# Five chunks accumulated per slice over unnormalised activations, with the root applied as the banks are copied

## The chip, the cores and the metric

The kernel runs on one core of a Trainium2 chip. The metric is the device time in microseconds of one execution, lower is better; a profile comes from one execution of its own.

## What is computed

Two transformer blocks on x of 256 tokens by 1024, float32. What concerns this change is the beginning of the first one:

```python
mod = c @ ada_w[l] + ada_b[l]
sh1, sc1, gt1, sh2, sc2, gt2 = [m[:, None, :] for m in jnp.split(mod, 6, axis=-1)]
h = rmsnorm(x, norm1_g[l]) * (1.0 + sc1) + sh1
p = h @ w_in[l]                       # 1024 -> 7168
xr, yr, q, k, v, ga, gb = jnp.split(p, cuts, axis=-1)
...
q = head_rmsnorm(q.reshape(b_, s_, ATT_HEADS, HEAD_DIM), q_norm_g[l])
k = head_rmsnorm(k.reshape(b_, s_, ATT_HEADS, HEAD_DIM), k_norm_g[l])
y_b = stick_breaking_attention(q, k, v)
```

rmsnorm divides each token's row by its root r = sqrt(mean(x^2) + eps). Behind these lines come a gated recurrence beside the attention, an output projection, a gated feed forward layer, and the second block: two attentions and 32 experts of two layers, of which each token takes four.

## The kernel before

Activations lie transposed: 1024 features as 8 slices k of 128 partitions, 256 tokens along the free side (`xT`, `hT`). Weights come in pieces of up to 1 MB through a ring of 17 slots; the SyncE queue issues the transfers in the order of `plan`, and each waits until the piece 17 places earlier has been used. c, the constants and the column vectors are issued by ScalarE's queue.

The order on every engine is written out by hand, and semaphores join them. At the start, ScalarE squares x, VectorE adds the squares, TensorE sums them over the features (L581), and ScalarE takes the root. For each slice k VectorE multiplies a piece of the modulation weights by c and sums it, one half for the shift and one for the scale (`first_modulation`, L1941), and multiplies x by the reciprocal root (L1946); ScalarE makes scale and shift of them and applies both (L1425), which is slice k of `hT` and raises `h`. TensorE then adds this slice's share to four chunks at once, the **slab** (L589): chunks ("qk", 0) to ("qk", 3), the eight heads' q, each 256 columns wide and in a bank of its own. Each later chunk is computed whole over the eight slices (`chunk`, L569): k in ("qk", 4) to ("qk", 7), then conv, v, gel and so on. This list is `main`; a chunk's place in it decides its bank and whom it waits for:

```python
n = self.main_at[key]
if n >= 3:
    _, sem, value = K.main[n - 3]
    e.wait_ge(sem, value)            # the chunk three places earlier is copied out
```

Every q and k chunk n is normalised by head: VectorE copies the bank (`qk_copy`, L1998), ScalarE squares it (L1433), TensorE sums (`qk_norm`, L612), ScalarE takes the root (L1439), VectorE takes the reciprocal (L2003) and multiplies (`qk_scale`, L2007 or L2009, and L2011 for q's factor 128^-0.5). VectorE's order is: copies 0, 1 and 2, scaling 0, copy 3, scaling 1, copy 4, scaling 2, some 128x8 operations of a softplus, copy 5, and so on. TensorE's attention scores of head 0 (L627) wait for all eight scalings.

The expert weights stream through the same ring at the end; their first transfers (L498) wait for the last pieces of the layers before them.

Of the kernel before, what the change touches and what calls it, by code (L numbers as in the profile page):

```python
# [15 lines left out]
S = 256  # L16
# [128 lines left out]
class Board:  # L145
# [36 lines left out]
    def lay_scratch(self):  # L182
# [16 lines left out]

        self.lt = [self.modc[:, 1, 8 * n:8 * n + 8] for n in range(5)]  # L200
        self.sq1 = [carve(512) for _ in range(4)]
        self.rst1 = carve(256)
        place[0] = 0
        self.qk = [carve(8, 256), carve(8, 256)]
        self.vv = carve(2, 1024)
        self.mix = carve(8, 256)
        self.Wt = [carve(512) for _ in range(10)]
        self.xp = carve(2, 260)
        self.xcs = [self.Wt[0], carve(512)]
# [78 lines left out]
    def lay_pieces(self):  # L288
# [10 lines left out]

        for k in range(8):  # L300
            ada(0, [k])
            plan.append((("slab", k), a["slab"][k], 1024))
        for n in range(4, 8):
            w_in(("qk", n), 8 + n)
        w_in(("conv", 0), 0)
        for c in range(4):
# [39 lines left out]
        self.done_at, n = {}, 0  # L346
        for key, _, _ in plan:
            if key == ("slab", 7):
                for c in range(4):
                    self.done_at[("qk", c)] = n + c + 1  # L350
                n += 3
            if key[0] not in ("b1", "ada"):
                n += 1
                self.done_at[key] = n
# [86 lines left out]
        return self.bank[3 if x == NE - 1 else 2]  # L441

    def main_bank(self, key):
        return self.bank[5 if key == ("qk", 3) else self.main_at[key] % 3]

    def second_bank(self, key):
        return self.bank[self.second_at[key] % 7]
# [12 lines left out]

    def modulation(self, i):

        return {0: (0, 0, "norm1", self.rst1), 1: (0, 24, "norm2", self.rst), 2: (1, 0, "pre_mix", self.rst),
                4: (1, 24, "pre_ffn", self.rst)}[i]


def sync_program(e, K):
# [86 lines left out]
def tensor_program(e, K):  # L554
# [28 lines left out]
    for k in range(8):  # L583
        v = landed(("slab", k))
        e.wait_ge(S.h, k + 1)
        for c in range(4):
            for j in range(2):
                o0 = c * 256 + j * 128
                ins = mm(K.main_bank(("qk", c))[:, 256 * j:256 * j + 256], v[:, o0:o0 + 128], K.hT[:, k, :],  # L589
                         start=(k == 0 and j == 0), stop=(k == 7), skip_group_check=True)  # L590
            if k == 7 or c == 3:
                ins.then_inc(S.piece_done, 1)
    e.wait_ge(S.ld_con2, 16)

# [9 lines left out]
    def chunk(key, h=None):  # L604
        v, b = main(key)
        tiles2(v, K.hT, b, h).then_inc(S.piece_done, 1)
# [4 lines left out]
            e.wait_ge(S.qk_rt, n - 1)  # L611
        mm(B[3 + n % 2][:, :], ones, K.Wt[2 * (n % 2)], start=True, stop=True).then_inc(S.qk_sum, 1)  # L612

    for n in range(4, 8):
        chunk(("qk", n))
        for m in range(2 * n - 8, 2 * n - 6):
            if m == 7:
                chunk(("conv", 0))
            qk_norm(m)

    def att_scores(h):
        b, q, k = B[3], K.qk[0][:, h, :], K.qk[1][:, h, :]
# [34 lines left out]
    for c in range(4):  # L657
        v, b = main(("v", c))
        for tt in range(2):
            for k in range(8):  # L660
                ins = mm(b[:, 256 * tt:256 * tt + 256], K.hT[:, k, tt * 128:(tt + 1) * 128],  # L661
                         v[:, k * 256:(k + 1) * 256], start=(k == 0), stop=(k == 7))
        ins.then_inc(S.piece_done, 1)
        chunk(("gel", c))
        att_step(2 * c)
        if c < 3:
            chunk(("conv", c + 1))
            att_step(2 * c + 1)
        rg = landed(("rg", c))
        e.wait_ge(S.xc, c + 1)  # L670
        if c:
            e.wait_ge(S.rg_th, c)
        xc = K.xcs[c % 2]
        for j in range(2):
            mm(B[5][:, 256 * j:256 * j + 256], rg[:, j * 128:(j + 1) * 128], xc[:, 256 * j:256 * j + 256], start=True,
               stop=True)
# [690 lines left out]
def scalar_program(e, K):  # L1367
# [31 lines left out]
                scale=K.mc[:, k:k + 1]).then_inc(S.h, 1)  # L1399


    e.dma_start(K.cb[:, :], a["cb1"]).then_inc(S.ld_cb, 16)
    e.dma_start(K.con[:, 0:256], a["consts"][:, 0:256]).then_inc(S.ld_col, 16)
    e.dma_start(K.col[:, :], a["cols"]).then_inc(S.ld_col, 16)
    e.wait_ge(S.consts, 3)
# [6 lines left out]
    e.wait_ge(S.act, done.n)  # L1412
    act(K.lt[0], K.lt[0], ACT.Exp, scale=-1.0).then_inc(S.coef, 1)
    table(ACT.Sqrt)
    norm_root(0, K.rst1)
    e.wait_ge(S.gain, 1)
    for k in range(8):
        e.wait_ge(S.ada_sum, 2 * k + 1)
        act(K.mc[:, 8 + k:9 + k], K.modc[:, 0, k:k + 1], ACT.Identity, bias=C("ada_b", k)).then_inc(S.act, done.one())
        e.wait_ge(S.ada_sum, 2 * k + 2)  # L1420
        act(K.mc[:, k:k + 1], K.modc[:, 0, 8 + k:9 + k], ACT.Identity, bias=K.mc[:, 16 + k:17 + k],
            scale=C("norm1", k)).then_inc(S.act, done.one())
        e.wait_ge(S.hn, k + 1)
        e.wait_ge(S.act, done.n)
        act(K.hT[:, k, :], K.hT[:, k, :], ACT.Identity, bias=K.mc[:, 8 + k:9 + k],  # L1425
            scale=K.mc[:, k:k + 1]).then_inc(S.h, 1)


    def qk_square(n):
# [426 lines left out]
def vector_program(e, K):  # L1856
# [69 lines left out]
    e.wait_ge(S.vec, done.n)  # L1926
    tt_(K.sq1[0][:, 0:256], K.sq1[0][:, 0:256], K.sq1[0][:, 256:512], ALU.add).then_inc(S.vec, done.one())
    e.wait_ge(S.ld_col, 32)
    stt(K.mc[:, 16:24], C("ada_b", 8, 8), 1.0, C("norm1", 0, 8), ALU.add, ALU.mult).then_inc(S.gain, 1)

    def first_modulation(k):

        i = K.at[("ada", 0, k)]
        v = K.piece(("ada", 0, k))
        for j in range(2):
            if k == 0 and j == 0:
                e.wait_ge(S.ld_ada, 16)
            else:
                e.wait_ge(S.ring[i % RING], 16 * (i // RING + 1))
            m, w = 8 * j + k, v[:, 1024 * j:1024 * j + 1024]  # L1940
            ins = stt(w, w, 1.0, K.cb[:, :], ALU.mult, ALU.mult, accum_out=K.modc[:, 0, m:m + 1])  # L1941
            ins.then_inc(S.ada_sum, 1)

    def first_scaled(k0, k1):
        for k in range(k0, k1):
            tt_(K.hT[:, k, :], K.xT[:, k, :], K.rst1, ALU.mult).then_inc(S.hn, 1)  # L1946

    e.wait_ge(S.ld_cb, 16)
    first_modulation(0)
    norm_end(0, K.rst1)  # L1950
    e.wait_ge(S.rstd, 1)
    first_scaled(0, 2)
    for k in range(1, 8):
        first_modulation(k)
        if k < 4:
            first_scaled(2 * k, 2 * k + 2)
    e.sem_inc(S.mod, 1)
    e.wait_ge(S.ld_con2, 16)

# [874 lines left out]
def lay_out(i):  # L2834
# [83 lines left out]
```

## Time and profile before

| | us |
|---|---|
| median of 3 runs | 1613.96 |
| lowest and highest | 1612.82, 1615.13 |
| the profiled execution | 1614.23 |
| its span, first to last instruction | 1612.3 |
| TensorE busy in it | 1558.4 (97%) |
| VectorE busy | 656.5 (41%) |
| ScalarE busy | 340.6 (21%) |

In the rows PE is TensorE, PEld its weight loads, DVE VectorE, ACT ScalarE, SP SyncE; q marks an engine's queue. Times count from the span's start. "a<-b" is output and inputs by their names in the program, and what stands in brackets at a row's end is the engine's idle time ahead of it and what ended it. TensorE's products are pipelined and their ends modelled, so the distance from start to start is the better measure. An f32 product appears as two instructions.

### The profile page before, as it was taken

The page shows a single profiled execution, that of the slowest core. Times are in us where ns is not written, and L with a number is a line of the kernel's source. Part 1 is how long each engine was busy: PE and PEld are TensorE (multiplying, and loading weights), DVE is VectorE, ACT ScalarE, POOL GpSimd, SP SyncE. Part 2 cuts the span into 40 slices and gives each one's busy share as a digit, 9 for nine tenths or more (in the row PEclk, how much of TensorE's full clock was granted, in tenths as well). Part 3 has the DMA queues.
Part 4 walks back from the last instruction along what each step waited for, and adds up shares of the span by engine and source line. Part 5 has one row for each costly group of instructions (what it writes and reads, how often), then busy time and mean ns, then how long its engine had stood idle before and what let it go on. Part 6 is the DMA issues. An engine that isn't in the chain of part 4 may idle for free.

```text
span 1612.3 us, 19170 instructions
## 1 busy us (share of the span) xinstructions
PE 1558.4 (97%) x7244; PEld 854.2 (53%) x7244; DVE 656.5 (41%) x1432; ACT 340.6 (21%) x658; POOL 0.2 (0%) x4
## 2 busy tenths in 40 slices
PE   6999999999999999899999999999999999999997
PEld 5788888888888886433333333333323333333222
DVE  6676862789810563432222232122222222222213
ACT  3236663432210244311010111010101010011001
POOL 0000000000000000000000000000000000000000
PEclk9999999999999999899999999999999999999999
DMA  9956793558963431599999999999999999999995
GB/s 385 420 194 241 261 349 139 191 190 346 409 269 128 139 130 53 198 419 421 421 421 421 420 421 421 421 421 421 420 422 422 421 421 421 421 421 421 421 421 222
DMA packets 78363, 544.93 MB, mean 338 GB/s; under 512 B 9104, under 2 KB 9872, under 8 KB 13616
## 3 DMA queue, kind: packets, MB, share of 16 engines
q1 hardware_dynamic: 76912, 541.66, 83.0%
q10 hardware_dynamic: 1344, 1.85, 0.4%
q8 instruction: 66, 1.08, 0.3%
q14 instruction: 41, 0.34, 0.1%
HBM read 542.43 MB, written 1.05 MB: 337 GB/s over the span
## 4 chain that ended last, share of the span: by engine, by line
PE 71%; SPq 16%; DMA 6%; DVE 4%; ACT 2%; issue 1%; ACTq 0%; DVEq 0%
PE bank L569 18%; PE bank L1164 17%; SPq L514 16%; PE bank L1230 9%; DMA ring<-in_w_mlp 5%; PE bank L744 5%; PE bank L1042 2%; PE bank L1273 2%; PE bank L589 2%; PE bank L708 2%; PE bank L1216 2%; PE bank L900 2%; PE bank L661 1%; PE bank L716 1%; PE bank L1102 1%
## 5 line engine op out<-in xcount | busy, mean ns | idle before, releaser
L1164 PE MATMUL bank<-ring,scr 128*64 128x512 f32 x1968 | 439.2, 596 | 13.2 <-DMA ring<-in_w_mlp 12.5
L569 PE MATMUL bank<-hT,ring 128*128 128x256 f32 x1440 | 315.4, 380 | 0.3
L569 PEld LDWEIGHTS bank<-hT,ring 128*128 128x128 f32 x1440 | 271.6, 190 | 41.5 <-issue 3.2
L1164 PEld LDWEIGHTS bank<-ring,scr 128*64 128x64 f32 x1968 | 135.8, 137 | 290.8 <-issue 244.0
L1230 PE MATMUL bank<-ring,hT 128*64 128x512 f32 x936 | 216.3, 596 | 5.0 <-DMA ring<-in_w_mlp 5.0
L2669 DVE TENSOR_SCALAR scr<-bank 128x256 f32<-128x256 f32 x64 | 27.0, 421 | 350.5 <-PE bank L1164 350.5
L1230 PEld LDWEIGHTS bank<-ring,hT 128*64 128x64 f32 x936 | 63.3, 136 | 129.5 <-issue 115.5
L1758 ACT ACTIVATE scr<-scr 128x256 f32<-128x256 f32 x64 | 26.7, 417 | 477.1 <-DVE scr L2669 477.1
L2546 DVE TENSOR_TENSOR scr<-bank,mc 128x512 f32<-128x512 f32 x33 | 22.8, 692 | 239.9 <-PE bank L1053 239.9
L1907 DVE SCALAR_TENSOR_TENSOR ring<-ring,con 128x1024 f32<-128x1024 f32 x80 | 94.5, 1219 | 0.0
L744 PE MATMUL bank<-scr,ring 128*128 128x256 f32 x384 | 83.1, 379 | 1.6 <-ACT scr L1574 1.6
L744 PEld LDWEIGHTS bank<-scr,ring 128*128 128x128 f32 x384 | 72.9, 190 | 11.9 <-ACT scr L1574 2.0
L1042 PE MATMUL bank<-scr 128*64 128x512 f32 x272 | 66.7, 612 | 0.6 <-DVE scr L2525 0.3
L1273 PE MATMUL bank<-hT,scr 128*128 128x512 f32 x128 | 59.2, 605 | 0.8 <-ACT hT L1819 0.8
L1804 ACT ACTIVATE hT<-bank 128x512 f32<-128x512 f32 x32 | 19.1, 597 | 170.4 <-PE bank L1058 164.0
L1273 PEld LDWEIGHTS bank<-hT,scr 128*128 128x128 f32 x128 | 23.0, 189 | 36.8 <-issue 35.1
L1042 PEld LDWEIGHTS bank<-scr 128*64 128x64 f32 x272 | 18.1, 139 | 42.2 <-issue 39.4
L2620 DVE COPY scr<-bank 64x256 f32<-64x256 f32 x64 | 27.0, 422 | 31.8 <-PE bank L1048 30.6
L589 PE MATMUL bank<-hT,ring 128*128 128x256 f32 x128 | 30.8, 407 | 3.9 <-ACT hT L1425 3.9
L1730 ACT ACTIVATE scr<-bank 128x512 f32<-128x512 f32 x32 | 19.1, 598 | 72.7 <-PE bank L1042 72.7
L2316 DVE SCALAR_TENSOR_TENSOR xT<-bank,modc,xT 128x256 f32<-128x256 f32 x8 | 3.5, 479 | 74.4 <-PE bank L744 74.4
L2766 DVE COPY hT<-bank 64x512 f32<-64x512 f32 x32 | 22.2, 694 | 26.9 <-PE bank L1230 26.9
(431 smaller groups left out, 1496.7 us busy)
## 6 DMA issues: line engine op xcount, KB each, us to landing
ring<-in_w_mlp SPq DMA_DIRECT2D x362, 1024.0 KB, 26.3
ring<-in_w_in SPq DMA_DIRECT2D x24, 1024.0 KB, 23.0
ring<-in_up SPq DMA_DIRECT2D x24, 1024.0 KB, 7.4
ring<-in_w_ada SPq DMA_DIRECT2D x24, 1024.0 KB, 7.2
con<-in_w_mlp SPq DMA_DIRECT2D x21, 1024.0 KB, 26.2
ring<-in_ada_w SPq DMA_DIRECT2D x16, 1024.0 KB, 5.1
ring<-in_down SPq DMA_DIRECT2D x12, 1024.0 KB, 15.9
ring<-in_ada SPq DMA_DIRECT2D x7, 1024.0 KB, 19.6
```

What stands on the lines that cost most here:

```text
L514: e.dma_start(K.moe_piece(i), src).then_inc(S.ring[K.moe_slot(i)], 16)
L569: ins = mm(b[:, 256 * j:256 * j + 256], v[:, k * 256 + j * 128:k * 256 + j * 128 + 128], rhs[:, k, :], start=(k == 0), stop=(k == 7))
L589: ins = mm(K.main_bank(("qk", c))[:, 256 * j:256 * j + 256], v[:, o0:o0 + 128], K.hT[:, k, :], start=(k == 0 and j == 0), stop=(k == 7), s ...
L708: ins = mm(B[c][:, 256 * j:256 * j + 256], v[:, k * 256 + j * 128:k * 256 + j * 128 + 128], K.mix[:, k, :], start=(k == 0), stop=(k == 7))
L744: ins = mm(b[j][:, 0:256], v[:, k * 256 + j * 128:k * 256 + j * 128 + 128], K.ff[:, kk * 8 + k, :], start=(kk == 0 and k == 0), stop=(kk = ...
L900: ins = mm(K.mixed(tt, hf)[:, :], K.yT[:, 4 * g + k, 128 * tt:128 * tt + 128], v[:, 512 * k:512 * k + 512], start=(g == 0 and k == 0), sto ...
L1042: ins = mm(B[3][64 * hf:64 * hf + 64, :], K.sel[c][:, tt, :], K.h4[:, tt, hf * 512:(hf + 1) * 512], start=(tt == 0), stop=(tt == 1), skip_ ...
L1164: ins = mm(HID[0][n][64 * hf:64 * hf + 64, :], K.xe[0][x % 2][:, xo:xo + 64], v[:, o0:o0 + 512], start=(x == 0 and k == 0), stop=(k == 7), ...
L1216: ins = mm(HID[1][n][64 * hf:64 * hf + 64, :], K.xe[1][x % 2][:, xo:xo + 64], v[:, o0:o0 + 512], start=False, stop=(k == 7), skip_group_ch ...
L1230: ins = mm((K.down_bank(x), B[1])[c][g:g + 64, :], K.aT[c][x % 2][:, 128 * q + 64 * hf:128 * q + 64 * hf + 64], v[:, j * 1024 + oh * 512:j ...
L1273: ins = mm(OUT[tt][oh][:, :], K.pairT[p % 2][oh][:, tt * 128:(tt + 1) * 128], K.ypair[oh], start=False, stop=False, skip_group_check=True)
L1907: ins = stt(w, w, 1.0, K.cb[:, :], ALU.mult, ALU.mult, accum_out=K.modc[:, n // 3, m:m + 1])
```

## The change

The root leaves the path to the slab. (x r^-1 scale + shift) W equals r^-1 ((x scale + shift r) W), so the slab now runs over `raw1` = x times scale plus shift times the root (`rt1`), and the copies of its banks multiply by the reciprocal root `rst`. In detail:

- ScalarE makes the scale of a slice and x times scale; VectorE makes the shift and adds shift times root (`first_shifted`). The scale's half of the modulation weights comes first. The reciprocal is taken once, behind slice 2. `hT`, which all later chunks read, is made out of `raw1` from slice 4 on (`first_normed`).
- The slab has five chunks: ("qk", 4) joins, in banks 5 and 6 for places 3 and 4, and its pieces are 1280 columns wide instead of 1024.
- The copies of chunks 0 to 4 are multiplications by `rst`; q's factor 128^-0.5 is put into the gain vector once, so L2011 goes.
- The first chunk behind the slab waits for all of `hT`; `qk_norm` 7 comes behind the first v chunk.
- c is issued by the SyncE queue, behind x and ahead of the weights.

The core of the diff:

```diff
         for k in range(8):
             ada(0, [k])
-            plan.append((("slab", k), a["slab"][k], 1024))
-        for n in range(4, 8):
+            plan.append((("slab", k), a["slab"][k], 1280))
+        for n in range(5, 8):
             w_in(("qk", n), 8 + n)
...
     def main_bank(self, key):
-        return self.bank[5 if key == ("qk", 3) else self.main_at[key] % 3]
+        n = self.main_at[key]
+        return self.bank[n + 2 if n in (3, 4) else n % 3]
...
+    e.dma_start(K.cb[:, :], a["cb1"]).then_inc(S.ld_cb, 16)
     for i, (key, src, n) in enumerate(K.plan):
...
-        for c in range(4):
+        for c in range(5):
             for j in range(2):
                 o0 = c * 256 + j * 128
-                ins = mm(K.main_bank(("qk", c))[:, 256 * j:256 * j + 256], v[:, o0:o0 + 128], K.hT[:, k, :],
+                ins = mm(K.main_bank(("qk", c))[:, 256 * j:256 * j + 256], v[:, o0:o0 + 128], K.raw1[:, k, :],
...
-    for n in range(4, 8):
-        chunk(("qk", n))
-        for m in range(2 * n - 8, 2 * n - 6):
-            if m == 7:
-                chunk(("conv", 0))
-            qk_norm(m)
+    e.wait_ge(S.hn, 8)
+    for n, key in enumerate((("qk", 5), ("qk", 6), ("qk", 7), ("conv", 0))):
+        chunk(key)
+        qk_norm(2 * n)
+        if n < 3:
+            qk_norm(2 * n + 1)
...
-    norm_root(0, K.rst1)
+    norm_root(0, K.rt1)
     e.wait_ge(S.gain, 1)
     for k in range(8):
         e.wait_ge(S.ada_sum, 2 * k + 1)
-        act(K.mc[:, 8 + k:9 + k], K.modc[:, 0, k:k + 1], ACT.Identity, bias=C("ada_b", k)).then_inc(S.act, done.one())
-        e.wait_ge(S.ada_sum, 2 * k + 2)
...
-        e.wait_ge(S.hn, k + 1)
         e.wait_ge(S.act, done.n)
-        act(K.hT[:, k, :], K.hT[:, k, :], ACT.Identity, bias=K.mc[:, 8 + k:9 + k],
-            scale=K.mc[:, k:k + 1]).then_inc(S.h, 1)
+        act(K.raw1[:, k, :], K.xT[:, k, :], ACT.Identity, scale=K.mc[:, k:k + 1]).then_inc(S.act, done.one())
...
-    def first_scaled(k0, k1):
-        for k in range(k0, k1):
-            tt_(K.hT[:, k, :], K.xT[:, k, :], K.rst1, ALU.mult).then_inc(S.hn, 1)
+    def first_shifted(k):
+
+        e.wait_ge(S.ada_sum, 2 * k + 2)
+        tt_(K.mc[:, 8 + k:9 + k], K.modc[:, 0, k:k + 1], C("ada_b", k), ALU.add).then_inc(S.vec, done.one())
+        e.wait_ge(S.norm_rt, 1)
+        e.wait_ge(S.act, 2 * k + 3)
+        e.wait_ge(S.vec, done.n)
+        stt(K.raw1[:, k, :], K.rt1, K.mc[:, 8 + k:9 + k], K.raw1[:, k, :], ALU.mult, ALU.add).then_inc(S.h, 1)
+
+    def first_normed(k):
+        e.wait_ge(S.h, k + 1)
+        tt_(K.hT[:, k, :], K.raw1[:, k, :], K.rst, ALU.mult).then_inc(S.hn, 1)
 
     e.wait_ge(S.ld_cb, 16)
-    first_modulation(0)
-    norm_end(0, K.rst1)
-    e.wait_ge(S.rstd, 1)
-    first_scaled(0, 2)
-    for k in range(1, 8):
+    for k in range(8):
         first_modulation(k)
-        if k < 4:
-            first_scaled(2 * k, 2 * k + 2)
+        first_shifted(k)
+        if k == 2:
+            e.reciprocal(K.rst, K.rt1).then_inc(S.rstd, 1)
+        if k > 3:
+            if k == 4:
+                e.wait_ge(S.rstd, 1)
+            for m in range(2 * k - 8, 2 * k - 6):
+                first_normed(m)
...
+        if n < 5:
+            rst = K.rst.unsqueeze(1).to_broadcast([128, 2, 256])
+            tt_(dst.rearrange("p (a b) -> p a b", a=2), src.rearrange("p (a b) -> p a b", a=2), rst,
+                ALU.mult).then_inc(S.qk_raw, 1)
+            return
+        e.tensor_copy(dst, src).then_inc(S.qk_raw, 1)
...
-            stt(dst, dst, C("qg"), rst, ALU.mult, ALU.mult).then_inc(S.vec, done.one())
-            e.wait_ge(S.vec, done.n)
-            ts_(dst, dst, 128.0 ** -0.5, None, ALU.mult).then_inc(S.qk, 1)
+            stt(dst, dst, K.mc[:, 24:25], rst, ALU.mult, ALU.mult).then_inc(S.qk, 1)
```

What stands on TensorE from the slab (L589) to the first convolution chunk; x64 is 64 products, `bank<-hT,ring` is a chunk, `bank<-scr,con` a norm sum. Before:

```order
L589 MATMUL bank<-hT,ring 128x256 x64
L569 MATMUL bank<-hT,ring 128x256 x16
L612 MATMUL bank<-scr,con 128x512 x2
L569 MATMUL bank<-hT,ring 128x256 x16
L612 MATMUL bank<-scr,con 128x512 x2
L569 MATMUL bank<-hT,ring 128x256 x16
L612 MATMUL bank<-scr,con 128x512 x2
L569 MATMUL bank<-hT,ring 128x256 x16
```

With the change (the lines have moved by two, L589 is L591 and so on):

```order
L591 MATMUL bank<-scr,ring 128x256 x80
L571 MATMUL bank<-hT,ring 128x256 x16
L614 MATMUL bank<-scr,con 128x512 x2
L571 MATMUL bank<-hT,ring 128x256 x16
L614 MATMUL bank<-scr,con 128x512 x2
L571 MATMUL bank<-hT,ring 128x256 x16
L614 MATMUL bank<-scr,con 128x512 x2
L571 MATMUL bank<-hT,ring 128x256 x16
```

One chunk of 16 products has moved into the slab, 64 to 80. The first norm sums still stand one chunk behind the slab, and each later chunk stands one norm pair closer to it: places 4, 5, 6 and 7 before, places 5, 6, 7 and 8 now.

On VectorE, from the last weight product of the slab to scaling 1, with the semaphores that each row waits for (piece_done: TensorE has finished the chunk; qk_rt: the root of the norm sum). Before:

```order
L1941 SCALAR_TENSOR_TENSOR ring,modc<-ring,con 128x1024 [waits w14] x2
L1998 COPY scr<-bank 128x512 [waits h,piece_done,ld_con2]
L1998 COPY scr<-bank 128x512 [waits piece_done] x2
L2003 RECIPROCAL scr<-scr 128x512 [waits qk_rt]
L2009 SCALAR_TENSOR_TENSOR scr<-scr,col 128x512 [waits vec,qk_sq]
L2011 TENSOR_SCALAR scr<-scr 128x512 [waits vec]
L1998 COPY scr<-bank 128x512 [waits piece_done]
L2003 RECIPROCAL scr<-scr 128x512 [waits qk_rt]
```

With the change (L2010 is the multiplying copy, L2018 the reciprocal, L2024 the product):

```order
L1941 SCALAR_TENSOR_TENSOR ring,modc<-ring,con 128x1024 [waits w14] x2
L1947 TENSOR_TENSOR mc<-modc,col 128x1 [waits ada_sum]
L1951 SCALAR_TENSOR_TENSOR scr<-scr,mc 128x256 [waits vec,act,norm_rt]
L1955 TENSOR_TENSOR hT<-scr,rst 128x256 [waits h] x2
L2010 TENSOR_TENSOR scr<-bank,rst 128x512 [waits piece_done,ld_con2]
L2010 TENSOR_TENSOR scr<-bank,rst 128x512 [waits piece_done] x2
L2018 RECIPROCAL scr<-scr 128x512 [waits qk_rt]
L2024 SCALAR_TENSOR_TENSOR scr<-scr,mc 128x512 [waits vec,qk_sq]
L2010 TENSOR_TENSOR scr<-bank,rst 128x512 [waits piece_done]
L2018 RECIPROCAL scr<-scr 128x512 [waits qk_rt]
```

The copies are now multiplications by `rst`, the separate multiplication behind each product is gone, and the last two normalisations of `hT` (L1955) stand ahead of the copies. Copy 3 stands behind scaling 0 in both.

## Rows read from the trace of the kernel before

**Rows 1.** The page: the chain that ended last, by engine
```profile
PE 71%; SPq 16%; DMA 6%; DVE 4%; ACT 2%; issue 1%; ACTq 0%; DVEq 0%
```

**Rows 2.** Timeline, start of the slab: start us, us, engine, line, operation
```profile
10.59 1.22 DVE L1941 SCALAR_TENSOR_TENSOR ring<-ring,con 128x1024 f32<-128x1024 f32 x1
11.73 1.22 DVE L1941 SCALAR_TENSOR_TENSOR ring<-ring,con 128x1024 f32<-128x1024 f32 x1
15.86 30.82 PE L589 MATMUL bank<-hT,ring 128*128 128x256 f32 x128 [3.93 <-ACT hT L1425]
```

**Rows 3.** Line L485, the first half weight piece: its issue and landing
```profile
L485 SPq DMA_DIRECT2D ring<-in_ada x1: 423/423/423, 1.7 to 1.7; - x1
...
DMA to landing us min/median/max: 8.1/8.1/8.1
```

**Rows 4.** Windows of TensorE: stretch, length, busy (instructions), granted clock, DMA share, GB/s
```profile
21.00:22.00 1.00, 1.00 (x4) 1.00 0.93 377
22.00:23.00 1.00, 1.00 (x7) 1.00 1.08 434
```

**Rows 5.** Timeline, the weight products of slices 3 and 7
```profile
22.48 1.23 DVE L1941 SCALAR_TENSOR_TENSOR ring<-ring,con 128x1024 f32<-128x1024 f32 x1 [0.71 <-DMA ring<-in_ada]
...
37.54 1.23 DVE L1941 SCALAR_TENSOR_TENSOR ring<-ring,con 128x1024 f32<-128x1024 f32 x1 [1.37 <-DMA ring<-in_ada]
```

**Rows 6.** Timeline, from the slab's end to the third chunk
```profile
46.52 7.07 PE L569 MATMUL bank<-hT,ring 128*128 128x256 f32 x32
53.43 1.88 PE L612 MATMUL bank<-scr,con 128*128 128x512 f32 x4
...
55.21 3.35 DVE L2003 RECIPROCAL scr<-scr 128x512 f32<-128x512 f32 x1 [8.66 <-ACT scr L1439]
58.68 0.75 DVE L2009 SCALAR_TENSOR_TENSOR scr<-scr,col 128x512 f32<-128x512 f32 x1
...
59.81 0.68 DVE L1998 COPY scr<-bank 128x512 f32<-128x512 f32 x1
...
60.53 0.63 ACT L1433 ACTIVATE scr<-scr 128x512 f32<-128x512 f32 x1 [4.26 <-DVE scr L1998]
...
63.77 7.07 PE L569 MATMUL bank<-hT,ring 128*128 128x256 f32 x32
...
65.60 3.35 DVE L2003 RECIPROCAL scr<-scr 128x512 f32<-128x512 f32 x1
```

**Rows 7.** Timeline, end of the scalings and first attention scores
```profile
81.81 0.75 DVE L2007 SCALAR_TENSOR_TENSOR scr<-scr,col 128x512 f32<-128x512 f32 x1
82.48 0.16 DVE L1977 TENSOR_TENSOR modc<-modc 128x8 f32<-128x8 f32 x1
...
97.06 0.75 DVE L2007 SCALAR_TENSOR_TENSOR scr<-scr,col 128x512 f32<-128x512 f32 x1
...
102.80 0.59 PE L627 MATMUL bank<-scr 128*128 128x256 f32 x2
...
107.94 0.56 DVE L2049 SCALAR_TENSOR_TENSOR scr<-bank,scr 128x384 f32<-128x384 f32 x1 [6.35 <-ACT scr L1456]
```

**Rows 8.** The page: a VectorE multiply that reads a bank, mean ns
```profile
L2546 DVE TENSOR_TENSOR scr<-bank,mc 128x512 f32<-128x512 f32 x33 | 22.8, 692 | 239.9 <-PE bank L1053 239.9
```

**Rows 9.** Timeline of TensorE at the router
```profile
657.83 1.32 PE L986 MATMUL bank<-con,scr 128*128 128x128 f32 x8 [2.38 <-DVE scr L2466]
```

**Rows 10.** Windows of TensorE around that pause
```profile
657.50:660.00 2.50, 1.95 (x14) 1.00 0.87 364
660.00:662.50 2.50, 2.50 (x13) 0.53 0.01 3
```

**Rows 11.** Windows of every engine: scalings, and the expert stream
```profile
60.00:80.00 20.00, 19.20 (x82) 15.08 (x81) 19.20 (x27) 4.94 (x8) 0.00 (x0) 1.00 1.02 420
676.00:1595.00 919.00, 898.97 (x4133) 305.66 (x4132) 232.51 (x546) 89.00 (x169) 0.00 (x0) 1.00 1.01 418
```

**Rows 12.** Waits of the SyncE queue: us in total, times, longest
```profile
SPq L498 <- PE bank L900: 54.5, 4, 31.3
```

More of the change, by code:

```diff
@@ L201, in lay_scratch @@
         self.sq1 = [carve(512) for _ in range(4)]
-        self.rst1 = carve(256)
         place[0] = 0
@@ L206, in lay_scratch @@
         self.mix = carve(8, 256)
+        self.raw1, self.rt1 = self.vv.rearrange("p a (b c) -> p (a b) c", b=4), self.mix[:, 0, :]
         self.Wt = [carve(512) for _ in range(10)]
@@ L348, in lay_pieces @@
             if key == ("slab", 7):
-                for c in range(4):
+                for c in range(5):
                     self.done_at[("qk", c)] = n + c + 1
-                n += 3
+                n += 4
             if key[0] not in ("b1", "ada"):
@@ L461, in modulation @@
     def modulation(self, i):
-        return {0: (0, 0, "norm1", self.rst1), 1: (0, 24, "norm2", self.rst), 2: (1, 0, "pre_mix", self.rst),
+        return {0: (0, 0, "norm1", self.rst), 1: (0, 24, "norm2", self.rst), 2: (1, 0, "pre_mix", self.rst),
                 4: (1, 24, "pre_ffn", self.rst)}[i]
@@ L585, in tensor_program @@
         e.wait_ge(S.h, k + 1)
-        for c in range(4):
+        for c in range(5):
             for j in range(2):
                 o0 = c * 256 + j * 128
-                ins = mm(K.main_bank(("qk", c))[:, 256 * j:256 * j + 256], v[:, o0:o0 + 128], K.hT[:, k, :],
+                ins = mm(K.main_bank(("qk", c))[:, 256 * j:256 * j + 256], v[:, o0:o0 + 128], K.raw1[:, k, :],
                          start=(k == 0 and j == 0), stop=(k == 7), skip_group_check=True)
-            if k == 7 or c == 3:
+            if k == 7 or c == 4:
                 ins.then_inc(S.piece_done, 1)
@@ L663, in tensor_program @@
         ins.then_inc(S.piece_done, 1)
+        if c == 0:
+            qk_norm(7)
         chunk(("gel", c))
@@ L1399, in modulate @@
                 scale=K.mc[:, k:k + 1]).then_inc(S.h, 1)
-    e.dma_start(K.cb[:, :], a["cb1"]).then_inc(S.ld_cb, 16)
     e.dma_start(K.con[:, 0:256], a["consts"][:, 0:256]).then_inc(S.ld_col, 16)
@@ L1928, in vector_program @@
     e.wait_ge(S.ld_col, 32)
+    ts_(K.mc[:, 24:25], C("qg"), 128.0 ** -0.5, None, ALU.mult).then_inc(S.vec, done.one())
     stt(K.mc[:, 16:24], C("ada_b", 8, 8), 1.0, C("norm1", 0, 8), ALU.add, ALU.mult).then_inc(S.gain, 1)
@@ L1934, in first_modulation @@
         v = K.piece(("ada", 0, k))
-        for j in range(2):
-            if k == 0 and j == 0:
+        for j in (1, 0):
+            if k == 0 and j == 1:
                 e.wait_ge(S.ld_ada, 16)
@@ L1939, in first_modulation @@
                 e.wait_ge(S.ring[i % RING], 16 * (i // RING + 1))
-            m, w = 8 * j + k, v[:, 1024 * j:1024 * j + 1024]
+            m, w = 8 * j + k, v[:, 1024 * (1 - j):1024 * (1 - j) + 1024]
             ins = stt(w, w, 1.0, K.cb[:, :], ALU.mult, ALU.mult, accum_out=K.modc[:, 0, m:m + 1])
             ins.then_inc(S.ada_sum, 1)
-    def first_scaled(k0, k1):
-        for k in range(k0, k1):
-            tt_(K.hT[:, k, :], K.xT[:, k, :], K.rst1, ALU.mult).then_inc(S.hn, 1)
-    e.wait_ge(S.ld_cb, 16)
-    first_modulation(0)
-    norm_end(0, K.rst1)
-    e.wait_ge(S.rstd, 1)
-    first_scaled(0, 2)
-    for k in range(1, 8):
-        first_modulation(k)
-        if k < 4:
-            first_scaled(2 * k, 2 * k + 2)
+    def first_shifted(k):
[8 more added lines that the diff above has]
+        tt_(K.hT[:, k, :], K.raw1[:, k, :], K.rst, ALU.mult).then_inc(S.hn, 1)
+    e.wait_ge(S.ld_cb, 16)
+    for k in range(8):
+        first_modulation(k)
+        first_shifted(k)
[6 more added lines that the diff above has]
+                first_normed(m)
     e.sem_inc(S.mod, 1)
@@ L1995, in qk_copy @@
         landed(("qk", n))
-        if n == 0:
-            e.wait_ge(S.h, 8)
-        e.tensor_copy(K.pair(K.qk[n // 4], n % 4), K.main_bank(("qk", n))[:, :]).then_inc(S.qk_raw, 1)
+        dst, src = K.pair(K.qk[n // 4], n % 4), K.main_bank(("qk", n))[:, :]
+        if n < 5:
[4 more added lines that the diff above has]
+        e.tensor_copy(dst, src).then_inc(S.qk_raw, 1)
     def qk_scale(n):
@@ L2855, in lay_out @@
     ada0 = np_("ada_w")[0][:, 0:2048].T.reshape(2, 8, 128, 1024)
-    o["ada0"] = np.ascontiguousarray(ada0.transpose(1, 2, 0, 3)).reshape(8, 128, 2048)
+    o["ada0"] = np.ascontiguousarray(ada0[::-1].transpose(1, 2, 0, 3)).reshape(8, 128, 2048)
     for n, w in (("ada_w", np_("ada_w")[0]), ("w_ada_2", np_("w_ada_2")[0])):
@@ L2859, in lay_out @@
     o["cb1"] = np.ascontiguousarray(np.broadcast_to(np_("c")[0][None], (128, 1024)))
-    o["slab"] = np.ascontiguousarray(np_("w_in")[0][:, 2048:3072]).reshape(8, 128, 1024)
+    o["slab"] = np.ascontiguousarray(np_("w_in")[0][:, 2048:3328]).reshape(8, 128, 1280)
     o["cb2"] = np.ascontiguousarray(np.broadcast_to(np_("c_2")[0][None], (128, 1024)))
```

## The prediction, made before the change was run

> **What bounds the kernel now.** I read the chain that ended last first: TensorE stands in 71% of it [rows 1]. It falls into two parts. From about 676 us to 1595 us the transfers run without a pause at 418 GB/s (share 1.01) [rows 11], so the expert weights set the pace there; but that stream can only start when TensorE gives its ring slots back, and the queue waited 54.5 us for the projection at L900 [rows 12]. So a TensorE delay ahead of it moves the whole stream, microsecond for microsecond. Before it, from about 16 us on, TensorE hardly stands still. The change touches the first 103 us; what counts is when TensorE starts head 0's attention scores (L627), 102.80 us [rows 7], since from there both kernels have the same work.
>
> In those 103 us the reader should see three things. First, the slab (L589) starts at 15.86 us [rows 2] and the next chunk at 46.52 us [rows 6], 30.66 us for 128 passes (an f32 product shows as two). A chunk of 32 passes takes 53.43 - 46.52 = 6.91 us [rows 6], 0.216 a pass, so the slab at full rate would be 27.6 us. The other 3.04 us are a slow beginning: 4 passes touch the slice 21 to 22 us, 7 the next [rows 4]. So the slab is bound by TensorE, not by its transfers. Second, VectorE, 19.20 of 20 us busy between 60 and 80 us [rows 11], works through eight q/k scalings: reciprocal, product, a bank copy. Third, the scalings end with the product at 97.06 us, 5 us before the scores want them, so now TensorE's own queue sets 102.80.
>
> **The change, part by part.**
>
> *Start of the slab.* Old path: two weight products from 10.59, reciprocal, x times rstd, ScalarE's scale and shift, slab at 15.86 [rows 2]. New path: scale half first, shift half second, while ScalarE does x times scale beside the second; then a 128x1 add and one 128x256 product on VectorE. Reciprocal and two multiplications leave the path. With the same start: 10.59 + 1.14 + 1.14 = 12.9 (a product begins 1.14 behind the one ahead of it), plus some 0.8, an estimate: a small add took 0.16 [rows 7], the 128x256 product is put at 0.5, under the 0.75 of one twice as wide [rows 6], the rest is handover. 13.7 us: gain 2.1. x now has its queue slot ahead of c, so its squares can end earlier; but the first weight half is issued at 1.7 and lands 8.1 later, 9.8 [rows 3], and that does not get earlier. This bounds the gain at 2.9. I take 13.3 us, gain 2.5. The Trainium skill ("DMA: Bandwidth & Descriptors", section on queues, rings and completion order) says each engine alternates between queues by packets; by it c no longer takes turns with x, which speaks for the upper bound. The trace of before cannot show the new order.
>
> *Width of the slab.* 160 passes instead of 128; 160 x 0.216 = 34.5, plus the same 3.04: end at 13.3 + 37.6 = 50.9 us. Transfers: a pair of pieces takes (37.54 - 22.48)/4 = 3.77 us now [rows 5]; 1.08 times the bytes gives 4.08, below TensorE's 20 x 0.216 = 4.3. The last weight piece would land near 39.7, its slice be ready near 42.7, and TensorE reach it at 46.6. VectorE's per-slice work (2.3 for the products, about 0.7 for add and product, 0.8 for two normalisations) stays under 4.08; the 128x256 reciprocal, half of the 3.35 us of a 512-wide one [rows 6], falls in the third slice with 3 us in hand. So all of these cost nothing, hidden by TensorE's backlog; without it each slice would cost its own lateness. The four ada_b activations leave ScalarE free: nothing. The multiplied bank copies: a 128x512 f32 multiply from a bank takes 692 ns [rows 8], a copy 0.68 us [rows 6]: nothing. The chunk that moved into the slab is gone behind it; TensorE's total is unchanged.
>
> *What is late next.* The norm sum of q pair 0 still comes one chunk behind the slab, in both kernels. But the slab now ends 4.4 us later, so it comes at 50.9 + 6.9 = 57.8, before at 53.43. From the norm sum the old rows count: reciprocal +1.78, product +3.47 (58.68), copy 3 +1.13 (59.81), and 0.72 from a copy's start to its reader on another engine (60.53) [rows 6]. The separate multiplication by 128^-0.5 is gone: from such a product to the next instruction is 0.67 (81.81 to 82.48 [rows 7]), not 1.13; saving 0.46, four times.
>
> The decisive piece is a wait that no line of the diff names. A chunk at place n of main waits for the copy of place n-3. Place 6 waits for copy 3, and VectorE does copy 3 only behind scaling 0, which needs the norm sum. In the old order two chunks lay between: place 6 began at 63.77, copy 3 at 59.81 [rows 6]. Now place 6 comes right behind norm sums 0 and 1 (1.72 us the pair: half of what 53.43 to 63.77 holds beside a chunk). TensorE is free at 59.5. Copy 3 begins at 57.8 + 1.78 + 3.47 + 0.67 = 63.7, its reader may go at 64.4. **TensorE stands still for 4.9 us.** The new banks 5 and 6 for places 3 and 4 do not help, since the rule waits by place. Behind the stalled matmul are norm sums 2 and 3; scaling 2 on VectorE waits for the first.
>
> *The clock.* After 2.38 us of idleness before 657.83 [rows 9] and sparse products behind it, the granted clock went from 1.00 (657.5 to 660) to 0.53 (660 to 662.5) [rows 10], the 1.2 GHz level instead of 2.4. Here the pause is twice that. The nearest price of a cold stretch is the slab's own, 3.04 us; the other bound is nothing. The fall may come late in the pause or after it (it came 4.7 us behind the start of the idleness), so I take 2.5. The Trainium skill ("TensorE: Matmul & The Clock Gate", section on HAM oscillation) warns that pauses between bursts make the next burst cold; it speaks against this change, and the row agrees, though with sparse work beside the pause. By the page the sum has this term, without the page's rule it ends 2.5 lower.
>
> *Sum.* Place 6: 64.4 + 6.9 + 2.5 = 73.8; scaling 2 starts at 75.6. In the old run it is 31.46 us from the reciprocal at 65.60 to the last product at 97.06 without a gap that counts; less 2 x 0.46 that is 30.5, and 0.8 to the scores: 75.6 + 30.5 + 0.8 = 106.9. TensorE alone would be there at 73.8 + 1.7 + 6.9 + 1.7 + 6.9 + 0.9 + 6.9 + 0.9 + 6.9 = 106.6, so VectorE sets it by a hair. Against 102.80: **+4.2 us** (rounding of the steps taken in). VectorE reaches the first convolution 9 us later than before, but had 6.35 us of waiting there for ScalarE's softplus [rows 7], and the scores are 4 later themselves: no further cost. The profiled execution took 1614.23 us (span 1612.3), the median is 1613.96; I put the difference on the median: **1618.2 us**.
>
> **The rivals.**
> - *The hold occurs, the clock stays up.* Speaks for it: the pause at 655 was followed by small products too, so the pause alone may not have done it. Place 6 ends at 71.3, scaling 2 starts at 73.1, scores at 104.5: +1.7, **1615.7 us**.
> - *Not slower: no hold at place 6.* If copy 3 were ready by 59.5, or the wait did not bind, scalings would run from 59.6 for 41.85 - 4 x 0.46 = 40.0 us, scores at 100.4: -2.3, **1611.6 us**. It decides at a copy 3 that begins before 58.8; VectorE's order, with scaling 0 ahead of it, speaks against it.
> - *The delay is absorbed.* Some later wait, of TensorE for ScalarE or at the stream's start, could hide it: **1614 us**. The rows show TensorE nearly without idle time in between, so little speaks for it.
>
> **How the numbers follow.** Hold and cold clock 0.60; hold alone 0.25; absorbed 0.10; no hold 0.05. The likeliest case alone: the gain at the start 2.1 to 2.9 and the clock 1.5 to 3.0 give +2.9 to +5.1, 1616.4 to 1619.5 with the runs' own spread near 1. Reaching to the hold-alone case and its spread, and to a clock that stays low longer, gives 1615.0 to 1620.4. What a measurement here can tell is about 0.2%, 3.2 us: slower than 1617.2 is most of the first case (0.53) and a little of the second; faster than 1610.7 needs no hold and more start gain than the landing allows.
>
> **What the new profile would show.** Slab from 13.3 to about 50.9 without TensorE waits; last slice ready well before 46; TensorE idle some 4.9 us ahead of the second chunk behind the slab, released by VectorE's copy of pair 3; granted clock 0.5 in the first microseconds after it; copies of 128x512 near 0.69 us; scores at 107. I am wrong if that idle time is missing, if the slab starts later than 13.8 or stalls for pieces, or if the 4 us at the scores are gone at 283 us, where the up projection begins.

## The result and the profile after

| | before | changed |
|---|---|---|
| median of 13 runs each | 1613.13 us | 1617.17 us |
| lowest to highest | 1612.17 to 1615.49 | 1616.15 to 1620.85 |
| ratio, 95% interval | | 1.0028 [1.0021, 1.0036] |
| the profiled execution | 1614.23 | 1617.17 |
| its span | 1612.3 | 1615.3 |

The changed kernel is slower: 4.0 us between the medians, and 0.28% by the ratio, which is taken over all the runs. Three of its 13 runs lie at 1620.6 to 1620.9 us, apart from the other ten, with the lowest mean granted clock of the thirteen (0.992); no profile fell on one of them, so what sets them apart stays open.

The start of the slab, from the timeline of the changed kernel (beside [rows 2]):

```profile
10.31 1.23 DVE L1941 SCALAR_TENSOR_TENSOR ring<-ring,con 128x1024 f32<-128x1024 f32 x1
...
11.51 1.23 DVE L1941 SCALAR_TENSOR_TENSOR ring<-ring,con 128x1024 f32<-128x1024 f32 x1
...
12.22 0.51 ACT L1425 ACTIVATE scr<-xT,mc 128x256 f32<-128x256 f32 x1
...
13.09 0.48 DVE L1951 SCALAR_TENSOR_TENSOR scr<-scr,mc 128x256 f32<-128x256 f32 x1
...
13.72 2.90 PE L591 MATMUL bank<-scr,ring 128*128 128x256 f32 x6 [2.32 <-DVE scr L1951]
```
These are the scale half and the shift half of the modulation products, x times scale on ScalarE beside the second, the shifted slice on VectorE, and the slab, which TensorE starts at 13.72 us instead of 15.86.

TensorE from the slab's end to the attention scores (beside [rows 6, 7]):

```profile
49.89 7.07 PE L571 MATMUL bank<-hT,ring 128*128 128x256 f32 x32
56.80 1.88 PE L614 MATMUL bank<-scr,con 128*128 128x512 f32 x4
63.54 9.38 PE L571 MATMUL bank<-hT,ring 128*128 128x256 f32 x32 [4.87 <-DVE scr L2010]
72.76 1.88 PE L614 MATMUL bank<-scr,con 128*128 128x512 f32 x4
...
105.89 0.70 PE L629 MATMUL bank<-scr 128*128 128x256 f32 x2 [0.19 <-DVE scr L2022]
```
Two things are to be seen. After the norm sums of pairs 0 and 1 the engine stands still for 4.87 us, and the bracket names the releaser: VectorE at L2010, the multiplying copy. And the chunk behind the pause lasts 72.76 - 63.54 = 9.22 us from start to start, where its neighbour took 56.80 - 49.89 = 6.91. The scores begin at 105.89, 3.09 later than before.

VectorE over the same stretch:

```profile
48.36 0.69 DVE L2010 TENSOR_TENSOR scr<-bank,rst 128x512 f32<-128x512 f32 x1 [0.17 <-PE bank L591]
58.58 3.35 DVE L2018 RECIPROCAL scr<-scr 128x512 f32<-128x512 f32 x1 [9.52 <-ACT scr L1438]
62.04 0.75 DVE L2024 SCALAR_TENSOR_TENSOR scr<-scr,mc 128x512 f32<-128x512 f32 x1
62.71 0.68 DVE L2010 TENSOR_TENSOR scr<-bank,rst 128x512 f32<-128x512 f32 x1
63.31 3.34 DVE L2018 RECIPROCAL scr<-scr 128x512 f32<-128x512 f32 x1
...
67.43 0.68 DVE L2010 TENSOR_TENSOR scr<-bank,rst 128x512 f32<-128x512 f32 x1
74.54 3.35 DVE L2018 RECIPROCAL scr<-scr 128x512 f32<-128x512 f32 x1 [6.43 <-ACT scr L1438]
...
105.09 0.75 DVE L2022 SCALAR_TENSOR_TENSOR scr<-scr,col 128x512 f32<-128x512 f32 x1
```
Copy 3 (62.71) stands behind scaling 0 (58.58 and 62.04), which had to wait for the norm sum. Copy 4 (67.43) is then done, but the third reciprocal starts only at 74.54, since the norm sum of pair 2 stands behind the slow chunk. From there to the last product at 105.09 VectorE does not wait.

Windows of TensorE in the changed kernel: stretch, length, busy time and instructions, granted clock, DMA share, GB/s:

```profile
16.00:17.00 1.00, 1.00 (x4) 1.00 1.05 439
17.00:18.00 1.00, 1.00 (x7) 1.00 1.06 442
60.00:61.00 1.00, 0.00 (x0) 1.00 1.10 440
61.00:62.00 1.00, 0.00 (x0) 0.63 1.05 436
62.00:63.00 1.00, 0.00 (x0) 0.50 1.01 418
67.00:68.00 1.00, 1.00 (x4) 0.50 1.03 418
68.00:69.00 1.00, 1.00 (x6) 0.96 0.95 385
```
The granted clock is 0.63 in the slice from 61 us and 0.50 in the next: it fell from its 2.4 GHz level to the 1.2 GHz level inside the pause, and rose at 68. In the slice from 67 us four passes are touched instead of six or seven. The slab has such a slow beginning too, four passes in the slice from 16 us and seven in the next. The clock column reads 1.00 in both slices, so that this was the lower level as well is read from the pace alone, which is that of the stretch at 0.50.

The up projection begins

```profile
286.27 4.05 PE L571 MATMUL bank<-hT,ring 128*128 128x256 f32 x16
```
at 286.27, 3.19 us later than before (283.08), so nothing of the delay is absorbed between the scores and there. The expert stream runs as before, and the queue's wait for the projection ahead of it is there too (beside [rows 11, 12]):

```profile
676.00:1595.00 919.00, 898.86 (x4131) 305.43 (x4130) 234.31 (x553) 89.42 (x170) 0.00 (x0) 1.00 1.01 418
```
```profile
SPq L500 <- PE bank L904: 56.2, 4, 31.3
```

### The profile page after: what moved, and what is told of

Same layout as the page of the kernel before. It is cut to its first block, busy times and chain, and to the rows that moved or that the text cites. A ratio compares the mean times of both kernels' runs of the same rounds, so it can differ in the third digit from the quotient of the medians.

```text
span 1615.3 us, 19175 instructions
## 1 busy us (share of the span) xinstructions
PE 1559.0 (97%) x7244; PEld 854.1 (53%) x7244; DVE 659.9 (41%) x1445; ACT 337.1 (21%) x650; POOL 0.2 (0%) x4
## 4 chain that ended last, share of the span: by engine, by line
PE 66%; SPq 17%; DMA 9%; DVE 5%; ACT 2%; issue 2%; ACTq 0%; DVEq 0%
PE bank L571 17%; SPq L516 16%; PE bank L1168 15%; DMA ring<-in_w_mlp 9%; PE bank L1234 8%; PE bank L748 5%; PE bank L591 2%; PE bank L1046 2%; PE bank L712 2%; PE bank L1220 2%; PE bank L1277 2%; PE bank L904 2%; DVE scr L2018 1%; PE bank L720 1%; PE bank L663 1%
## 5 line engine op out<-in xcount | busy, mean ns | idle before, releaser
L571 PE MATMUL bank<-hT,ring 128*128 128x256 f32 x1408 | 310.6, 382 | 5.1 <-DVE scr L2010 4.9
L571 PEld LDWEIGHTS bank<-hT,ring 128*128 128x128 f32 x1408 | 267.0, 191 | 46.5 <-issue 8.4
L748 PE MATMUL bank<-scr,ring 128*128 128x256 f32 x384 | 83.1, 379 | 1.6 <-ACT scr L1573 1.6
L748 PEld LDWEIGHTS bank<-scr,ring 128*128 128x128 f32 x384 | 72.9, 190 | 11.9 <-ACT scr L1573 2.0
L591 PE MATMUL bank<-scr,ring 128*128 128x256 f32 x160 | 36.3, 391 | 2.3 <-DVE scr L1951 2.3
L591 PEld LDWEIGHTS bank<-scr,ring 128*128 128x128 f32 x160 | 31.4, 197 | 7.5 <-DMA ring<-in_slab 3.0
```

Of the source, the lines that this page charges most:

```text
L571: ins = mm(b[:, 256 * j:256 * j + 256], v[:, k * 256 + j * 128:k * 256 + j * 128 + 128], rhs[:, k, :], start=(k == 0), stop=(k == 7))
L748: ins = mm(b[j][:, 0:256], v[:, k * 256 + j * 128:k * 256 + j * 128 + 128], K.ff[:, kk * 8 + k, :], start=(kk == 0 and k == 0), stop=(kk = ...
```

## The experiments

Each was run beside the kernel before. Its median was 1612.91 us (33 runs) beside filled_pause, gate_by_bank, four_chunks and norms_early, and 1613.47 us (12 runs) beside the other four; the ratios are to these runs, and the ratio of the changed kernel is to the 13 runs above. Where there is one run alone, only its profile is used. "Scores" is the start of the first attention scores in its profile.

| kernel | median us, runs | ratio to before, 95% | scores | up projection |
|---|---|---|---|---|
| before | 1613.13, 13 | | 102.80 | 283.08 |
| changed | 1617.17, 13 | 1.0028 [1.0021, 1.0036] | 105.89 | 286.27 |
| filled_pause | 1614.68, 11 | 1.0009 [1.0000, 1.0018] | 103.71 | 284.08 |
| gate_by_bank | 1611.03, 11 | 0.9983 [0.9974, 0.9992] | 99.89 | 280.26 |
| four_chunks | 1610.59, 11 | 0.9983 [0.9974, 0.9992] | 100.19 | 280.45 |
| norms_early | 1609.64, 11 | 0.9977 [0.9968, 0.9986] | 98.52 | 278.79 |
| norms_only | 1608.58, 8 | 0.9971 [0.9961, 0.9982] | 99.04 | 279.30 |
| folded_gain | 1612.75, 1 | | 101.56 | 281.83 |
| x_first | 1611.90, 1 | | 101.23 | 281.48 |
| changed_again | 1617.36, 1 | | 105.95 | 286.32 |

**gate_by_bank.** The hold taken away without moving anything: places 6 and 7 wait for the copies of the places whose banks they reuse.

```diff
-            _, sem, value = K.main[n - 3]
+            _, sem, value = K.main[n - 6 if n in (6, 7) else n - 3]
```

> The changed kernel, but places 6 and 7 of main wait for the copies of places 0 and 1, whose banks they reuse, and no longer for copies 3 and 4. Theory 1 (the hold at place 6 and the low clock behind it make the loss): the hold of 4.87 us and the low clock go, VectorE's scalings run through, the scores start near 99.7 us instead of 105.9, time about 1610.0 us, 3 below the kernel before and 7 below the changed one. Theory 2 (the slab's later end delays the first norm sum by 3.4 us, and VectorE's chain behind it sets the scores whatever place 6 waits for): scores near 105, time about 1616 us.

```profile
57.34 1.88 PE L614 MATMUL bank<-scr,con 128*128 128x512 f32 x4
59.06 7.07 PE L571 MATMUL bank<-hT,ring 128*128 128x256 f32 x32
...
99.89 0.70 PE L629 MATMUL bank<-scr 128*128 128x256 f32 x2 [0.99 <-DVE scr L2022]
```
The second chunk (59.06) follows the norm sums (57.34) directly, and the pause is gone. The scores start at 99.89, 6.0 us earlier than in the changed kernel, although the slab ended half a microsecond later here (50.43). VectorE's chain is now what is left: 0.99 us of wait at the scores. This bears out theory 1 in place and in size at the scores (99.7 was expected); a chain that starts at the same time and sets 105 in any case is ruled out. The median lies 1.9 us below the kernel before in the same session, where the changed kernel lay 4.0 above it: 5.9 us between the two. It is 1.0 us above the 1610.0 expected.

**filled_pause.** The wait stays, the idleness goes.

```diff
+        if n == 1:
+            for _ in range(5):
+                mm(B[7][:, :], ones, K.con[:, 0:512], start=True, stop=True)
         chunk(key)
```

> The changed kernel with five products of constants of 128x512 into bank 7, which nobody reads then, issued ahead of the wait at place 6 (4.3 us of work in the pause). It leaves the wait as it is. Theory 1 (the pause lets the clock fall, which costs 2.3 us of the loss): granted clock 1.0 throughout, place 6 still starts near 63.5 us but takes 6.9 instead of 9.2, scores near 103.8, time about 1615.0 us, 2 below the changed kernel. Theory 2 (VectorE's chain sets the scores and the cold chunk is hidden): scores stay at 105.9, 1617.2 us.

```profile
58.59 4.45 PE L620 MATMUL bank<-con 128*128 128x512 f32 x10
63.62 7.14 PE L571 MATMUL bank<-hT,ring 128*128 128x256 f32 x32 [0.57 <-DVE scr L2013]
70.60 1.88 PE L614 MATMUL bank<-scr,con 128*128 128x512 f32 x4
...
103.71 0.70 PE L632 MATMUL bank<-scr 128*128 128x256 f32 x2 [0.17 <-DVE scr L2025]
```
```profile
62.00:63.00 1.00, 1.00 (x3) 1.00 0.97 401
...
64.00:65.00 1.00, 1.00 (x7) 1.00 0.98 410
```
The filling products run in the pause, the chunk starts at 63.62 as before, but takes 70.60 - 63.62 = 6.98 us, at a granted clock of 1.00. The scores come 2.2 us earlier than in the changed kernel. So the fallen clock was worth 2.2 us at the scores, and 2.3 by the medians, each against the kernel before beside it. The hold itself is the rest. From the slab's end to the scores it is 56.00 us in the changed kernel, 53.74 with the pause filled and 49.46 in gate_by_bank, so 2.3 us go with the clock and 4.3 with the hold.

**four_chunks.** The new arithmetic without the fifth chunk:

```diff
-            plan.append((("slab", k), a["slab"][k], 1280))
+            plan.append((("slab", k), a["slab"][k], 1024))
...
-        for c in range(5):
+        for c in range(4):
...
-        if n < 5:
+        if n < 4:
```

and the chunk and norm orders of the kernel before.

> The changed kernel with the slab at four chunks and the orders of the kernel before; x ahead of c, the new arithmetic, the multiplying copies and the folded gain stay. Theory 1 (the new arithmetic gives its gain at the start and only the fifth chunk brings the hold): slab from 13.7 us, no pause behind it, scores between 98.2 and 99.6, time 1608.5 to 1610 us. Theory 2 (the new arithmetic itself costs, on VectorE between the slices or in the copies): 1613 us or more.

```profile
13.59 12.36 PE L590 MATMUL bank<-scr,ring 128*128 128x256 f32 x48 [2.39 <-DVE scr L1949]
26.98 18.15 PE L590 MATMUL bank<-scr,ring 128*128 128x256 f32 x80 [1.02 <-DVE scr L1949]
44.96 7.08 PE L570 MATMUL bank<-hT,ring 128*128 128x256 f32 x32
...
100.19 0.59 PE L629 MATMUL bank<-scr 128*128 128x256 f32 x2
```
```profile
22.03 1.74 DVE L1960 RECIPROCAL rst<-scr 128x256 f32<-128x256 f32 x1
...
26.35 0.48 DVE L1949 SCALAR_TENSOR_TENSOR scr<-scr,mc 128x256 f32<-128x256 f32 x1
```
There is no pause behind the slab, and the kernel is faster than before, so the new arithmetic is not what made the changed kernel slower. But it is not free here: with four chunks TensorE's backlog is too short. The reciprocal at 22.03 us delays slice 3 on VectorE, TensorE stands for 1.02 us until 26.98, and the next 80 passes take 44.96 - 26.98 = 17.98 us instead of 17.3. So both expectations were missed a little: the scores come at 100.19 and not at 98.2 to 99.6, and the median is 1610.59 us and not 1608.5 to 1610. In the changed kernel the fifth chunk covers this: its 160 passes run without a wait.

**norms_early.** gate_by_bank, and norm sums moved ahead:

```diff
-    for n, key in enumerate((("qk", 5), ("qk", 6), ("qk", 7), ("conv", 0))):
-        chunk(key)
-        qk_norm(2 * n)
-        if n < 3:
-            qk_norm(2 * n + 1)
+    qk_norm(0)
+    qk_norm(1)
+    for key, norms in ((("qk", 5), (2,)), (("qk", 6), (3, 4)), (("qk", 7), (5,)), (("conv", 0), (6,))):
+        chunk(key)
+        for m in norms:
+            qk_norm(m)
```

> gate_by_bank with norm sums 0 and 1 right behind the slab and the others each moved ahead by about a chunk. Theory 1 (with the hold gone VectorE's chain of eight scalings is what is left at the scores, and it starts as early as the first norm sum): chain from 51.7 us, no wait at the scores, they start near 98.2 us, time about 1608.5 us, 1.5 below gate_by_bank. Theory 2 (TensorE sets the scores once the hold is gone): the same as gate_by_bank.

The scores start at 98.52 without a wait (98.2 expected), 1.4 us ahead of gate_by_bank, and the medians differ by 1.4 too (1609.64, where 1608.5 was expected). The intervals of the ratios overlap, so for the time alone this second step is likely, not shown; the profiles show the wait at the scores gone.

**norms_only.** The same moved norm sums, with the wait by place as it was.

> The changed kernel with norm sums 0 and 1 right behind the slab and the others each ahead by about a chunk, and every place waiting for the copy three places earlier as it did. Theory 1 (the hold came only because place 6 stood right behind norm sum 0): scaling 0 starts near 51.7 us, copy 3 near 55.8, long before place 6 wants it at 59, so no hold and no low clock; scores near 98.3, time about 1609.5 us, the same as with the wait by bank. Theory 2 (the wait by place itself is what costs): a hold of some microseconds stays and the time is 1613 or more.

```profile
50.74 1.88 PE L614 MATMUL bank<-scr,con 128*128 128x512 f32 x4
52.45 7.07 PE L571 MATMUL bank<-hT,ring 128*128 128x256 f32 x32
...
60.22 7.07 PE L571 MATMUL bank<-hT,ring 128*128 128x256 f32 x32
...
99.04 0.59 PE L630 MATMUL bank<-scr 128*128 128x256 f32 x2
```
```profile
52.52 3.35 DVE L2019 RECIPROCAL scr<-scr 128x512 f32<-128x512 f32 x1 [2.62 <-ACT scr L1439]
...
56.65 0.68 DVE L2011 TENSOR_TENSOR scr<-bank,rst 128x512 f32<-128x512 f32 x1
```
The norm sum at 50.74 lets scaling 0 start at 52.52 and copy 3 at 56.65; place 6 finds it done and starts at 60.22 behind one norm sum. From the slab's end to the scores it is 48.30 us, the same as in norms_early; the scores are later than the 98.3 expected because the slab ended later (50.74). So the rule by place costs nothing here once the norm sums that copy 3 waits for stand a chunk further ahead. Of the two repairs, the order alone is enough. Its median, 1608.58 us, is the lowest here, 4.9 us below that of the kernel before in the same session (1613.47); against norms_early the intervals overlap.

**x_first.** The kernel before with the load of c moved behind x on the SyncE queue.

> The kernel before with x loaded ahead of c on the SyncE queue and nothing else. Theory 1 (most of the 2.1 us gained at the start is the shorter path, some is the transfer order): first weight product near 10.3 us instead of 10.59, slab near 15.5 instead of 15.86, time 0 to 0.5 us below. Theory 2 (the order of the transfers brings the gain): slab near 14 us.

```profile
10.24 1.19 PE L582 MATMUL bank<-scr,con 128*128 128x256 f32 x2 [10.24 <-DVE scr L1927]
15.54 29.59 PE L590 MATMUL bank<-hT,ring 128*128 128x256 f32 x128 [4.11 <-ACT hT L1425]
```
The slab starts at 15.54 instead of 15.86, where theory 2 had 14. So most of the 2.1 us gained at the start is the shorter path: 0.3 us go with the transfer order by this one profile, which is no more than the spread of the slab's start over the six profiles with five chunks (13.47 to 13.78 us), and about 1.8 with the path. The time of this one run, 1.6 us below the kernel before where 0 to 0.5 was expected, says nothing more, since the slab's slow beginning was shorter too (it ended 29.42 us after its start, before 30.66).

**folded_gain.** The kernel before with 128^-0.5 in the gain.

> The kernel before with 128^-0.5 folded into the q gain, nothing else. Theory 1 (VectorE's chain has 5 us in hand at the scores, but norm sum 5 waits 0.8 us for it): that wait goes, scores near 101.9 us instead of 102.8, VectorE's last product near 95.4 instead of 97.06. Theory 2 (it is off the path altogether): scores at 102.8.

```profile
70.50 1.88 PE L612 MATMUL bank<-scr,con 128*128 128x512 f32 x4
72.22 7.07 PE L569 MATMUL bank<-hT,ring 128*128 128x256 f32 x32
...
101.56 0.59 PE L627 MATMUL bank<-scr 128*128 128x256 f32 x2
```
Norm sums 4 and 5 run together at 70.50 and the chunk follows at 72.22, where it began at 73.46 before; the 0.8 us of wait is gone. VectorE's last product starts at 95.01 us (95.4 expected). The scores come 1.24 us earlier and the slab ended 0.17 earlier, so some 1.1 us come from the folding: the separate multiplication was on the path, which the prediction had not counted for the kernel before.

**changed_again.** The changed kernel once more.

> The changed kernel once more, to see what of its times comes from the clock. Theory 1: hold of 4.9 us, low clock behind it again, scores between 105 and 108 us depending on how long the slab's beginning and place 6 run at the low clock. Theory 2 (the clock fell by chance in the first profile): place 6 takes 6.9 us.

```profile
49.90 7.07 PE L571 MATMUL bank<-hT,ring 128*128 128x256 f32 x32
...
63.55 9.46 PE L571 MATMUL bank<-hT,ring 128*128 128x256 f32 x32 [4.86 <-DVE scr L2010]
72.84 1.88 PE L614 MATMUL bank<-scr,con 128*128 128x512 f32 x4
...
105.95 0.70 PE L629 MATMUL bank<-scr 128*128 128x256 f32 x2 [0.17 <-DVE scr L2022]
```
Pause, slow chunk (9.29 us) and scores are the same within 0.1 us. The clock fell in both profiles of this kernel, so theory 2 is out.

## Why the prediction was right

- *The hold at place 6.* Forecast: TensorE idle for 4.9 us, released by copy 3. Measured 4.87, with that releaser, and gate_by_bank and norms_only show it to be the cause: take it away by a different wait or by a different order, and 6 to 7 us go at the scores, the clock's share with them. gate_by_bank is also the prediction's rival without a hold: scores at 99.89 and 1611.03 us, where that rival had 100.4 and 1611.6.
- *The clock.* Forecast 2.5 us, measured 9.22 - 6.91 = 2.31. The fall came 2.6 us behind the end of the norm sums (56.80 + 1.88 = 58.68, and 0.63 as the mean of the slice from 61 puts it at 61.3), not 4.7; filled_pause shows that the idleness is what lets it fall. By the warning of the Trainium skill ("TensorE: Matmul & The Clock Gate", section on HAM oscillation) this was to be expected, and the trace agrees: the granted clock was 0.50 behind a pause of 4.87 us.
- *The start.* Forecast 13.3 us, measured 13.72, at the lower bound of the gain (2.1). x did come earlier with c behind it (ScalarE's squares of its second half began at 7.46 us, before at 7.99), but the first weight half was issued 0.5 later, behind c, and landed at 10.2, not at the 9.8 that I took. The first product began at 10.31, only 0.28 earlier than before; in changed_again VectorE waited 0.25 us for that landing.
- *The slab's slow beginning.* Forecast unchanged at 3.04 us. Measured 36.17 - 34.5 = 1.6: the pace rose at about 17 us and not 22, [rows 4] against the windows above. This term was wrong, and its length is not steady: over the six profiles with five chunks the slab takes 36.17 to 37.10 us. The later start (0.4) and the shorter beginning (1.4) pull opposite ways, and the slab ended at 49.89, forecast 50.9. That is the 1.0 us by which the sum was off at the scores.
- *The scores.* Forecast 106.9, measured 105.89. The steps from the slab's end agree: third reciprocal 24.65 us behind it (forecast 24.7), last product 30.55 behind that (30.5). VectorE sets the scores by a hair, as forecast: TensorE waits 0.19 us for its last product.
- *Little cost in the copies and in the slices.* The copies take 0.69 us, before 0.68. The slices were ready in time, but with less in hand than the prediction had: slice 3 at 27.6 us, when by my estimate (49.89 less five slices of 4.32) TensorE wanted it at 28.3, and slice 7 at 44.2 against 45.6, where the forecast had 42.7 against 46.6. four_chunks shows that this needed the fifth chunk's cover.
- *Nothing absorbed.* +3.09 at the scores, +3.19 at the up projection, +3.0 in the span. VectorE's last product came 8.0 us later, but its wait ahead of the first convolution shrank from 6.35 to 1.52 us, which took that up. The medians say 4.0, and this is nearer to the forecast 4.2 than the 3.1 that the change moved the scores by. The rest is within what the last section shows to vary between executions, so that part of the closeness is luck.
- *Not in the prediction:* the wait of norm sum 5 in the kernel before. The folding alone would have given it 1.1 us, so the changed kernel loses more to the hold than the difference of the two shows: without hold and cold chunk (gate_by_bank) it stands 1.9 us below the kernel before at the median.

## What to carry to other kernels

When work moves from one chunk to the stage ahead of it, read each remaining wait by the place it names and not by the buffer it protects: an unchanged rule "wait for the copy three places back" came to stand right behind the work that this copy waits for. TensorE's total of work was unchanged and its start 2.1 us earlier, but at one hand-over inside the chain it stood still for 4.87 us, of which 4.3 reached the scores, and the cold chunk behind it took 2.31 more. A pause that cannot be removed may be filled with useless products; moving the short ones (here the norm sums) ahead was better here, since it removed the pause and started the other engine's chain earlier.

## What else the runs showed of the hardware

The distance from the up projection's start to the end of the span differs between profiles of these kernels although the work is the same: 1329.0 us in the changed kernel (span 1615.3 less 286.27), 1331.4 in gate_by_bank, 1327.2 in norms_only. It goes with the granted clock at the router, where products are small and pauses frequent. The windows of 640 to 700 us of gate_by_bank and of norms_only, with the mean granted clock in the fifth column:

```profile
640.00:700.00 60.00, 55.63 (x234) 0.86 0.63 245
```
```profile
640.00:700.00 60.00, 55.31 (x253) 0.94 0.71 281
```
A mean of 0.86 over these 60 us is 17 us at the lower level, 0.94 is 7 us; the other profiles lie at 0.86 to 0.91 (0.91 for the changed kernel). In the ten profiles the distance is 1327.2 us at 0.94, 1327.7 to 1329.1 at 0.91, 1329.2 twice at 0.89, 1330.9 and 1331.4 at 0.86. In gate_by_bank and norms_only it can be seen where the 4.2 us arise. Eight passes of 128x512 of the output projection, just ahead of the router, take 5.38 us in gate_by_bank (L904, from 648.90) and 3.68 in norms_only (L905, from 647.94). From the router's transposes behind them (656.71 and 654.05) to the second group of 16 expert passes (674.95 and 670.07) it is 18.24 and 16.02 us. The two differences, 1.7 and 2.2 us, are 3.9 of the 4.2. So a stage hundreds of microseconds behind the change moves the time by up to 4 us, as much as the change does. That the clock orders the profiles was measured; why it stays at the lower level longer in one execution than in another was not.
